# Off-diagonal weights of the recurrent heads: each chunk's 32 keys against its own eight queries, in the chunk's column group

## What is computed

```python
def step(S, blk):                      # one chunk of c = 32 tokens
    qc, kc, lc, vc = blk
    b = jnp.cumsum(lc, axis=1)
    decay = jnp.exp(jnp.where(tri, b[:, :, None] - b[:, None, :], -jnp.inf))
    att = jnp.einsum('bthk,bshk,btshk->bhts', qc, kc, decay)
    o = (jnp.einsum('bhts,bshv->bthv', att, vc)
         + jnp.einsum('bthk,bhkv->bthv', qc * jnp.exp(b), S))
    ...
```

## Time and profile before

| | us |
|---|---|
| median of 3 runs | 1676.44 |
| lowest, highest | 1675.94, 1677.15 |
| the profiled execution, its own time | 1672.02 |
| span of its records | 1670.2 |
| TensorE busy in the span | 1522.2 (91%) |
| chain that ended last: TensorE, DMA, VectorE | 50%, 40%, 6% |

### The profile page before, as it was taken

How to read it: one execution, slowest core, us unless ns; L and a number is a source line. 1 busy time by engine, 2 the same in 40 slices (tenths; PEclk the granted TensorE clock), 3 DMA queues, 4 the chain that set the end, 5 groups by cost and what they waited for, 6 DMA issues and landing times.

```text
span 1670.2 us, 20165 instructions
## 1 busy us (share of the span) xinstructions
PE 1522.2 (91%) x8100; PEld 675.0 (40%) x8100; DVE 619.8 (37%) x1142; ACT 284.8 (17%) x646; POOL 48.3 (3%) x62
## 2 busy tenths in 40 slices
PE   7999999979999989789999899989989988989996
PEld 3545555544544655533333333333333333333332
DVE  2065785443240432633332234233233223423325
ACT  3113235342220331200000000000000000000002
POOL 3000000001010000000000000000000000000000
PEclk9998999999999999889999999999999999999999
DMA  7311220359452268479999999999999999999992
GB/s 243 133 52 51 78 99 3 140 178 348 164 213 94 76 251 345 140 293 427 428 429 428 428 427 428 429 427 427 428 428 429 429 428 427 429 427 430 428 426 89
DMA packets 69640, 499.98 MB, mean 299 GB/s; under 512 B 6912, under 2 KB 7472, under 8 KB 45008
## 3 DMA queue, kind: packets, MB, share of 16 engines
q1 hardware_dynamic: 58704, 468.47, 68.0%
q0 software_dynamic: 7760, 23.92, 4.1%
q10 hardware_dynamic: 3120, 6.82, 1.1%
HBM read 491.97 MB, written 11.14 MB: 301 GB/s over the span
## 4 chain that ended last, share of the span: by engine, by line
PE 50%; DMA 40%; DVE 6%; ACT 2%; issue 1%; SPq 1%; ACTq 0%; DVEq 0%; POOLq 0%
DMA ring<-w 38%; PE psum L2701 11%; PE psum L2088 11%; PE psum L2074 8%; PE psum L2640 4%; PE psum L2180 3%; PE psum L2655 1%; PE psum L2059 1%; DVE ring L1440 1%; PE psum L2430 1%; PE psum L2447 1%; PE psum L2228 1%; DMA ring<-w_in 1%; PE psum L2106 1%; PE psum L2209 1%
## 5 line engine op out<-in xcount | busy, mean ns | idle before, releaser
L2640 PE MATMUL psum<-ring,r_c 128*64 128x512 f32 x1504 | 341.5, 602 | 27.6 <-DMA ring<-w 26.3
L2701 PE MATMUL psum<-ring,r_c 128*64 128x512 f32 x1024 | 238.4, 615 | 53.4 <-DMA ring<-w 39.3
L2640 PEld LDWEIGHTS psum<-ring,r_c 128*64 128x64 f32 x1504 | 110.8, 138 | 250.9 <-issue 191.8
L1959 DVE TENSOR_TENSOR r_x<-r_x,psum 128x1024 f32<-128x1024 f32 x64 | 78.1, 1221 | 267.9 <-PE psum L2655 267.9
L2701 PEld LDWEIGHTS psum<-ring,r_c 128*64 128x64 f32 x1024 | 77.6, 140 | 192.1 <-issue 120.6
L2074 PE MATMUL psum<-r_h,ring 128*128 128x512 f32 x320 | 140.6, 600 | 1.9 <-ACT r_h L879 1.9
L1977 DVE TENSOR_SCALAR r_c<-r_c 128x512 f32<-128x512 f32 x32 | 13.5, 423 | 299.8 <-ACT r_c L1246 299.8
L2655 PE MATMUL psum<-r_c,early 64*128 64x512 f32 x512 | 122.3, 608 | 0.8 <-ACT r_c L1253 0.8
L1246 ACT ACTIVATE r_c<-psum 128x512 f32<-128x512 f32 x32 | 19.1, 597 | 588.9 <-PE psum L2640 588.9
L2088 PE MATMUL psum<-ring,r_h 128*128 128x512 f32 x256 | 114.0, 605 | 1.0 <-DMA ring<-w_in 1.0
L1979 DVE RECIPROCAL r_c<-r_c 128x512 f32<-128x512 f32 x32 | 107.3, 3353 | 1.1
(11 more groups left out here) (371 smaller groups left out, 1372.0 us busy)
## 6 DMA issues: line engine op xcount, KB each, us to landing
ring<-w SPq DMA_DIRECT2D x158, 2048.0 KB, 23.7
r_mix<-w SPq DMA_DIRECT2D x16, 2048.0 KB, 26.6
r_h<-w SPq DMA_DIRECT2D x16, 2048.0 KB, 27.4
ring<-w_in SPq DMA_DIRECT2D x6, 2048.0 KB, 9.7
ring<-cache_mem_v SPq DMA_DIRECT2D x8, 1024.0 KB, 10.0
ring<-cache_mem_k POOLq DMA_DIRECT2D x8, 1024.0 KB, 8.1
ring<-cache_moba_v SPq DMA_DIRECT2D x24, 256.0 KB, 5.6
ring<-w_xk SPq DMA_DIRECT2D x2, 2048.0 KB, 7.8
```

Source lines behind the costliest of these rows:

```text
L1959: return dve.tensor_tensor(x, x, psum_t[:, bank:bank + 2, :].rearrange("p a n -> p (a n)"), ALU.add)
L2640: ins = pe.matmul(psum[2 + 2 * u + m][CAP * half:CAP * (half + 1), :], xT[:, k, CAP * u:CAP * (u + 1)], (first_row(2 + m, kk) if first els ...
L2701: ins = pe.matmul(psum[7][CAP * half:CAP * (half + 1), :], heT[u][:, k % 4, CAP * (k // 4):CAP * (k // 4 + 1)], place[:, kk, 512 * half:51 ...
```

## The change

For every j and every tile the one product is replaced by four, one per chunk c of the tile. Each takes the 32 keys of its chunk as stationary operand and the chunk's own eight queries as moving operand, and writes to the PSUM partitions 32c to 32c+31, which puts the stationary operand into column group c of the array. Consecutive products therefore go to column groups 0, 1, 2, 3 in turn. The result is the same block of the bank that the mask picks out; what stood elsewhere in the bank is no longer written. VectorE, ScalarE and the queues have the same instructions as before.

```diff
                 for j in range(3):
                     for i in range(NT):
-                        c = slice(P * j + NS * i, P * j + NS * (i + 1))
-                        pe.matmul(s[:, c], kb[j][:, tok(i)], hgt["qo"][:, c], start=True, stop=True)
+                        for c in range(P // CH):
+                            at = P * j + NS * i + SUB * c
+                            keys = slice(P * i + CH * c, P * i + CH * (c + 1))
+                            pe.matmul(s[CH * c:CH * (c + 1), at:at + SUB], kb[j][:, keys], hgt["qo"][:, at:at + SUB],
+                                      start=True, stop=True, skip_group_check=True)
```

## The result

| | before | changed |
|---|---|---|
| median, us | 1676.32 (6 runs) | 1666.93 (6 runs) |
| lowest, highest | 1674.85, 1682.64 | 1664.26, 1669.09 |
| profiled execution, its own time; its span | 1672.02; 1670.2 | 1666.10; 1664.3 |

The ratio of changed to before is 0.9937, 95% interval 0.9923 to 0.9951. The change is faster by 0.63%, about 10 us. The two profiled executions differ by 5.9 us, as forecast, but that agreement is an accident, as the following shows.

What follows compares the result with a forecast made beforehand. TensorE's passes in `weights_inside`, filled by loads of 128 weight columns, were taken to bound heads 0, 1 and 3; savings of 3.17 + 1.36 + 0 + 1.36 = 5.9 us gave a median of 1670.5 us, range 1668.5 to 1674.8.

Steps and rivals of the forecast that it cites:

- Which heads are on the path: Heads' weights_inside: heads 0, 1 and 3 pass on their savings; head 2 saves 0, its wait growing to 3.50 us.
- Spacing of the passes at full clock: L2108's 96 passes per head: 14 ns apart, 1.34 us, saving 1.36 us a head (bounds 1.74 and 0.11).
- Head 0: L2108 of head 0 at the low clock: 20 ns a pass, 1.92 us for 5.09, saving 3.17 us.
- The sum of 5.9 us around the heads: Savings of heads 0 to 3: 3.17 + 1.36 + 0 + 1.36 = 5.9 us less.
- The term for the passes: Heads 0, 1 and 3: fewer, closer passes at full clock save 1.36 us each, 4.1 us.
- The term for the clock: Head 0's saving beyond 1.36 us, 1.8 us, its low stretch and the clock's return moving earlier, counted whole.
- Nothing in the edit scales with: Profiled execution lies 4.4 us below the runs' median; the edit leaves that gap, so the median becomes 1670.5.
- Rival A: The longer wait before head 3 makes the clock fall there, costing 2.5 us; total 1673.0 us; chance 0.2.
- Rival B: TensorE's sequencer keeps L2108's passes no closer than 27 ns; total saving 2.7 us, 1673.7 us; chance 0.15.
- rival C: Column groups don't work beside each other in L2108: 37 ns a pass, 3.7 us more, 1680.1 us; chance 0.08.

Runs made afterwards that it cites:

- head2_only: Kernel before with the small products in head 2 only, the other heads keeping the 12 larger products; 1676.98 us, ratio 0.9998 to before.
- head0_only: Kernel before with the small products in head 0 only, heads 1 to 3 keeping the 12 larger products; 1673.13 us, ratio 0.9981 to before.
- before_twice: The kernel before, unchanged, measured and profiled a second time; ratio 1.000 to before, mean 1676.8 us over 11 runs.
- Both fillers: Changed kernel plus useless products behind L2108 in each head, dense (two of 512 columns) or thin; 1671.88 and 1672.79 us, ratios 0.9967 and 0.9972 to before.
- thin filler: Changed kernel plus eight useless products of 128-column weights and 32 moving columns behind L2108 in each head; 1672.79 us, ratio 0.9972 to before.
- large_and_small: Each head does the old 12 large products into an unused bank, then the 48 small ones; 1676.14 us, ratio 1.0003 to before.
- diagonal_too: Changed kernel with the diagonal product (L2099) also cut into 32-key chunks in column groups; 1665.75 us, ratio 0.9931 to before.

## Why the prediction was too small

- **Which heads are on the path**: right. Heads 0 and 3 start with VectorE's L1418, head 1 follows TensorE, head 2 ends in the wait (3.92 us in the profile, 3.5 forecast), and head2_only measured its worth at nothing. Nothing behind the heads gave the saving back either: the stage of the experts is 954.9 us before and 954.8 after.
- **Spacing of the passes at full clock**: the term was mis-sized. The forecast took 14 ns between 10 and 27; it measured 8.4 ns, below the low end. The weight of "96 in a row is three times as long" was wrong: the run of 96 keeps the pace of L2315's 32. Heads 1 and 3 save 1.9 us each for 1.36 forecast, when at full clock: 1.1 us more in all.
- **Head 0**: forecast 3.17 us, on the assumption that it lies in a low stretch and L2108 takes 1.92 us there. At full clock, where the profiles of the changed kernel, of head0_only and the second one of the kernel before have it, the edit itself saves 1.9. At the low clock L2108 measured 1.32 us (head 3 of the changed kernel), for 5.09: 3.8 us. Measured alone over 12 runs: 3.2 us by the ratio, 3.6 by the means.
- **The sum of 5.9 us around the heads: this is the step that failed**, in two of its terms. The stage from L2099 of head 0 to L2209 became 8.9 us shorter, in both pairs of profiles. The term for the passes was 1.36 us for each of three heads, 4.1 us; the stage less half of its low-clock time shows 5.5. The term for the clock was what head 0 was to save beyond that, 3.17 - 1.36 = 1.8 us: the low stretch was to stay at head 0 and as long as it was, only moved forward ("I count it whole"). Instead low-clock time in the stage fell from 10.2 to 3.4 us, of which half, 3.4 us, is time. 4.1 + 1.8 is the 5.9 forecast, 5.5 + 3.4 the 8.9 measured.
- **"Nothing in the edit scales with" the 4.4 us between profiled execution and median**: this held, as far as the runs show. The first profiled execution had 72.9 us of low-clock time, near the mean of 75.0. It was short in stages that the edit doesn't touch: 138.8 us ahead of the heads, where the 14 profiles go up to 142.0, and 461.5 us behind L2209, where they go up to 467.9. The median before, 1676.32, less 8.9 is 1667.4, and 1666.93 was measured. The means over all runs differ by 10.4 us with an error of 0.6; the 1.5 us beyond 8.9 are located nowhere. In the last two columns of the table the 10.4 is 4.7 (half of 75.0 - 65.5) plus 5.7, but the two add up by construction, and low-clock time at the experts costs nothing, so 4.7 us is more than the clock is shown to give. The two profiled executions differ by the 5.9 forecast only because the changed one was 2.9 us longer in parts that weren't edited: luck.
- **Rival A, the clock falls at head 3**: it came true in the profile (0.50 from 240.6 to 244.0). From L2099 of head 3 to L2180 or L2183 it is 10.38 us before and 10.02 changed, 0.4 less for the 1.9 that full clock would give, so it cost 1.5 us in this pair, for 2.5 priced. Against the kernel before it isn't a loss, because that has such a fall at head 3 in other executions, and a longer one (6.8 us in before_twice), and more low-clock time over all its runs. The prediction named that possibility and didn't weigh it.
- **Rival B (27 ns)** and **rival C (37 ns)** are excluded by the 8.4 ns. For B the prediction quoted the Trainium skill, TensorEngine Tiling (Array Packing), section Instruction Overhead: about 60 cycles of overhead per matmul, and no tiling factor from a dimension that is small already. As an estimate by this section of the Trainium skill, passes would have been at least 25 ns apart. This case's traces disagree where groups alternate (8.4 ns), and come near it (28 ns) where one group has 12 products in a row. For C it quoted the Trainium skill, TensorE: Matmul & The Clock Gate, section Step-by-step: what each phase is for, with about 62 ns per MATMUL when the hardware decoder is off. A whole product of two passes takes 17 ns here, so that rate did not bind; whether the decoder was on, no run here shows.

Left open: why the small products leave TensorE less at the low clock. Both fillers show that it isn't the time saved, and the thin filler that the filler's shape doesn't matter; large_and_small came out between. The low-clock times of single stages rest on one or two profiles of each kernel, and diagonal_too, with small products in every head, had 10.2 us like the kernel before. Whether the stretch of L2106 pulls the clock down, or L2108 holds it up, wasn't separated.

## What to carry to other kernels

A product of which only blocks are wanted can be cut into blocks of 32 stationary columns and become cheaper (0.81 us for 2.70 here), if consecutive products go to different column groups; put them in a row in one group and the gain is gone (2.64 us). When stretches of thin TensorE work lie between dense ones, read the granted clock of several executions before trusting one, and take granted clock and time together, stage by stage: where TensorE bounds the time, half of the low-clock time is lost (the stage of the heads), and where transfers bound it, nothing that shows (the stage of the experts). A difference between two profiled executions is worth little until it is split into the edited stage and the rest. Saving time on an engine that then waits is worth nothing, which one row of the timeline (the wait in front of the next step) tells in advance.

## What was not expected of the hardware

- 96 passes with 32-column weights in four column groups in turn start 8.4 ns apart at full clock, over the whole run, and 14 ns apart at the low clock, where the large passes take 112 and 212 ns.
- 8 or 32 moving columns make no difference there (8.4 and 8.6 ns); in one column group the same passes take 28 ns.
- The low-clock time of this kernel changed by 9 to 10 us of 75 with an edit of 8 us of TensorE work, and stayed changed when the time was filled up again.
- The stage of the experts took 954.1 to 955.1 us with 22.2 to 33.3 us of it at the low clock.
